# Projections of unnormalised tiles, the norm's inverse root applied to their results, and one sum over the squares

## What is computed

```python
def rms_norm(x, g):
    y = x * lax.rsqrt(jnp.mean(x * x, axis=-1, keepdims=True) + EPS)
    return y * g

for i in range(2):
    y = rms_norm(h, mix_norm[i])
    x_lru, g_lru, q, k, v, g_ret, u_sgu, v_sgu, g_sgu = split(y @ w_in[i])
    lru_out = rg_lru(conv(x_lru), ...)          # 4 taps, gates, a scan over the tokens
    ret_out = retention(q, k, v, ...)           # 6 heads, rotary q and k
    sgu_out = spatial_gating(u_sgu, v_sgu, ...)
    mixed = concatenate([lru_out * silu(g_lru), ret_out * silu(g_ret), sgu_out * silu(g_sgu)])
    h = h + mixed @ w_out[i]
    z = rms_norm(h, ple_norm[i])
    h = h + sigmoid(z @ w_ple_gate[i]) * (p[i] @ w_ple_proj[i])
h = rms_norm(h, final_norm)                     # then attention, then the experts
```

## Time and profile before

| | us |
|---|---|
| median of 3 runs (2720.45 to 2722.91) | 2721.89 |
| the profiled execution | 2722.76 |
| span of its trace | 2720.9 |
| PE busy / DVE busy / ACT busy / POOL busy | 2549.7 / 1837.7 / 1333.7 / 731.6 |
| layers 0 and 1 | 0 to 1070 |
| modulation and attention | 1070 to 1445 |
| experts | 1500 to the end |

### The profile page before, as it was taken

One profiled execution on the slowest core, in us unless ns is written; L12 is line 12 of the kernel. 1 busy time (PEld: TensorE's weight loads), 2 busy tenths in 40 slices (PEclk: granted clock), 3 DMA queues, 4 the chain that ended last, 5 costly groups with the idle time before them and its releaser, 6 DMA issues.

```text
span 2720.9 us, 32767 instructions
## 1 busy us (share of the span) xinstructions
PE 2549.7 (94%) x11541; PEld 2001.7 (74%) x11541; DVE 1837.7 (68%) x1658; ACT 1333.7 (49%) x1233; POOL 731.6 (27%) x402
## 2 busy tenths in 40 slices
PE   4999999989999988989896799999999999999995
PEld 2777787657777865678665688888888888888884
DVE  5478631264875123038524799999999999999995
ACT  3252233233322232123323577777777777777773
POOL 2333265233323632004321221122222121222120
PEclk8999999889999989999996899999999999999998
DMA  4233232132322323643102899999999999999993
GB/s 181 67 127 93 63 93 85 39 109 78 124 70 78 93 62 114 229 145 93 55 1 87 320 367 373 370 374 371 368 369 370 365 371 373 371 373 365 369 367 110
DMA packets 105359, 573.61 MB, mean 211 GB/s; under 512 B 14288, under 2 KB 14432, under 8 KB 55472
## 3 DMA queue, kind: packets, MB, share of 16 engines
q1 hardware_dynamic: 94416, 540.32, 53.4%
q0 software_dynamic: 10432, 31.81, 4.6%
q10 hardware_dynamic: 432, 0.40, 0.1%
HBM read 560.42 MB, written 24.12 MB: 215 GB/s over the span
## 4 chain that ended last, share of the span: by engine, by line
PE 90%; DVE 5%; ACT 1%; DMA 1%; DVEq 1%; issue 1%; POOL 0%; ACTq 0%; SPq 0%; POOLq 0%
PE ps L1465 87%; PE ps L1149 2%; DVE scr L1951 1%; DVEq L1955 1%; DVE scr L1931 1%; PE ps L623 0%; DMA pieces<-in_pieces 0%; POOL pieces_split L2142 0%; DMA scr<-in_positions 0%; DMA mix<-acc_rows 0%; PE ps L659 0%; DMA acc_rows<-rows,lst 0%; DVE scr L940 0%; DVE w_split L1276 0%; PE ps L1401 0%
## 5 line engine op out<-in xcount | busy, mean ns | idle before, releaser
L1276 DVE TENSOR_TENSOR w_split<-raw,w_split 128x2048 fp32r<-128x2048 f32 x386 | 877.6, 2288 | 54.3 <-ACT w_split L1228 43.4
L1465 PE MATMUL ps<-y_split,pieces_split 128*128 128x512 f32 x3600 | 854.8, 398 | 43.7 <-DVE y_split L1947 40.3
L1465 PEld LDWEIGHTS ps<-y_split,pieces_split 128*128 128x128 f32 x3600 | 682.6, 191 | 207.7 <-issue 44.7
L1228 ACT ACTIVATE w_split<-raw 128x2048 fp32r<-128x2048 f32 x386 | 736.3, 1917 | 197.3 <-PE ps L1465 177.3
L1465 PE MATMUL ps<-w_split,rows_T 128*128 128x512 f32 x3096 | 752.1, 394 | 1.9 <-DVE rows_T L1282 1.9
L1465 PEld LDWEIGHTS ps<-w_split,rows_T 128*128 128x128 f32 x3096 | 575.8, 189 | 118.8 <-DVE rows_T L1282 2.5
L2142 POOL TENSOR_TENSOR pieces_split<-pieces,pieces_split 128x1024 fp32r<-128x1024 f32 x172 | 420.0, 2445 | 878.9 <-ACT pieces_split L1713 571.0
L1713 ACT ACTIVATE pieces_split<-pieces 128x1024 fp32r<-128x1024 f32 x138 | 146.2, 1059 | 516.6 <-PE ps L1465 467.7
L1465 PE MATMUL ps<-w_split,hidden_T 128*128 128x512 f32 x1536 | 363.1, 392 | 1.7 <-DVE hidden_T L1282 1.7
L1465 PEld LDWEIGHTS ps<-w_split,hidden_T 128*128 128x128 f32 x1536 | 285.9, 188 | 72.1 <-DVE hidden_T L1282 13.9
L1340 POOL COPY rows_i<-slot_tokens 128x1 int32 (+1 forms) x34 | 59.2, 1742 | 409.4 <-PE ps L1149 375.5
(11 more groups left out here) (241 smaller groups left out, 2071.0 us busy)
## 6 DMA issues: line engine op xcount, KB each, us to landing
raw<-in_w_moe SPq DMA_DIRECT2D x386, 1024.0 KB, 7.4
pieces<-in_pieces SPq DMA_DIRECT2D x237, 512.0 KB, 3.7
acc_rows<-in_zeros POOLq DMA_DIRECT2D x5, 512.0 KB, 14.0
hT<-in_xT SPq DMA_DIRECT2D x8, 256.0 KB, 7.7
h_rows<-scr SPq DMA_DIRECT2D x4, 512.0 KB, 3.2
mix<-acc_rows SPq DMA_DIRECT2D x4, 512.0 KB, 5.0
out_T<-hT SPq DMA_DIRECT2D x8, 256.0 KB, 2.1
scr<-in_decay POOLq DMA_DIRECT2D x1, 1536.0 KB, 10.5
```

Source lines behind the costliest of these rows:

```text
L1228: nc.scalar.activation(wsp[:, p % SPLIT, 0], raw[:, p % RAW, :], ACT.Copy).then_inc(high, 3 if p == 1 else 1)
L1276: nc.vector.tensor_tensor(wsp[:, p % SPLIT, 1], raw[:, p % RAW, :], wsp[:, p % SPLIT, 0].bitcast(F32), ALU.subtract).then_inc(low, 3 if p ...
L1465: return pe.matmul(out, lhsT, rhs, start=start, stop=stop)
```

## The change

1. The tiles that are projected are `h * gain`, without the norm's factor. `gained_high` (ACT) and `gained_low` (DVE) make the two parts straight from `hT`.
2. The factor `rn` (the inverse root, the same on all partitions) is applied to results: `scale_gate` on DVE multiplies each gate's bank by `rn` before ACT's tanh; the convolution's first step multiplies xl by `rn` on its way out of PSUM, in place of ACT's copy; q and k by cos and sin tables that are multiplied by `rn` once (`ncos`, `nsin`); v and vs as the scale of ACT's copies, for which PE turns `rn` into columns by four tiny transposes into an A bank of their own (`rt`, placed between i2 and v0.0 in A's order) and ACT copies them to `rT`; u by a multiplication of the gate's product; g by `scale_ple`.
3. The first three projections of a norm go side by side over the tiles (`side_by_side`: xl0..xl2, g0..g2), nine matmuls for each tile.
4. DVE adds the eight squared tiles (`add_square`), and one matmul sums over the partitions (`norm_sum`), within the side-by-side part (after tile 7; in layer 1's opening after tile 3).
5. At the start: x and pieces are loaded in turns; the preparation of constants (decay rates, rotary tables) goes from before the first norm to between layer 0's convolutions; POOL issues its constant loads after its first weight pieces.
6. p and `w_ple_proj` come by one DMA into `work`; the raw places then hold only the next layer's pieces, and the next layer's first four pieces are split during g4..g7. The small products stand between g4..g7 and after them.

```diff
@@ layer_pieces
-    out += col(a, *(f"g{i}" for i in range(DK)))
-    out += [(f"ple{i}", False, v, f"p{DK - 1}") for i in range(4)]
+    out += col(v, "g0", "g1", "g2") + col(a, *(f"g{i}" for i in range(3, DK)))
@@ a_order
             a_order += [f"{w}{3 * g + m}" for m in range(3) for w in ("r", "i")]
+            a_order += ["rt"] if g == 0 else []
             a_order += [f"v{g}.{t}" for t in range(ST)]
@@ TensorE
-            for k in range(DK):
-                next_sum(-1, k)
+            def norm_sum(layer, g, n):
+                pe.wait_ge(sq_added, n)
+                pe.wait_ge(A.free, A.reusable(layer, g) if layer >= 0 else 1)
+                mm(ps[:, A.bank(g), :], ones[:], sq_sum, True, True).then_inc(A.full, 1)
...
+                def side_by_side(pool, names, first, sums):
+                    ws = [wps[:, L_AT[g] % A_SPLIT].rearrange("p c (k n) -> p c k n", k=DK) for g in names]
+                    for g in names:
+                        high_of(L_AT[g])
+                        low_of(L_AT[g])
...
+                    for k in range(DK):
+                        at_ = layer * 2 * DK + first + k + 1
+                        pe.wait_ge(yh_ready, at_)
+                        for g, w in zip(names, ws):
+                            mm(ps[:, pool.bank(g), :], w[:, 0, k, :], ys[:, 0, k, :], k == 0, False)
+                            mm(ps[:, pool.bank(g), :], w[:, 1, k, :], ys[:, 0, k, :], False, False)
+                        sums(k)
+                        pe.wait_ge(y_ready, at_)
+                        for g, w in zip(names, ws):
+                            m = mm(ps[:, pool.bank(g), :], w[:, 0, k, :], ys[:, 1, k, :], False, k == DK - 1)
...
+                def opening_sum(k):
+                    if k == (DK - 1 if layer == 0 else 3):
+                        norm_sum(layer - 1, "next", 2 * layer + 1)
+                side_by_side(A, ("xl0", "xl1", "xl2"), 0, opening_sum)
+                for name, _, pool, g in LAYER[3:12]:
+                    project(pools[pool], g)
@@ ScalarE
-                    nc.scalar.activation(mix[:, tile, :], full(V, g), ACT.Tanh, scale=0.5).then_inc(th_ready, 1)
+                    act.wait_ge(scaled, layer * 16 + i + 1)
+                    nc.scalar.activation(mix[:, tile, :], ps[:, V.bank(g), :], ACT.Tanh, scale=0.5).then_inc(th_ready, 1)
...
                     ahead("gl5" if g == 0 else "gr1")
                     for m in range(3):
                         act.wait_ge(la_ready, layer * 6 + 3 * g + m + 1)
                         nc.scalar.activation(mix[:, 6 + m, :], mix[:, 9 + m, :], ACT.Exp)
                         nc.scalar.activation(mix[:, 9 + m, :], mix[:, 9 + m, :], ACT.Tanh).then_inc(at_ready, 1)
+                    if g == 0:
+                        nc.scalar.activation(rT, full(A, "rt")[:, 0:8], ACT.Copy)
+                        act.drain().then_inc(A.free, 1)
@@ VectorE
-                r = inverse(7, std_ready, layer * NSTD + 8, std)
-                normalised(lambda k: p_("ple_norm", k), r, layer * 2 * DK + DK)
+                    if m >= 2:
+                        gained_low(m - 2, layer, DK, "ple_norm")
+                    if m >= 5:
+                        add_square(m - 4, layer * NSQ + 14, 14)
...
+                for i in range(3):
+                    conv(i)
+                if layer == 0:
+                    prep_one_plus()
+                scale_gate("gl0", 0)
+                conv(3)
+                silu2("gl0", 0, 0)
+                conv(4)
+                if layer == 0:
+                    prep_rate()
+                conv(5)
+                if layer == 0:
+                    prep_angles()
+                gates([f"gl{i}" for i in range(1, 6)], lambda i: 1 + i, 1)
```

More of the change, by code:

```diff
@@ L26 @@
 AX = mybir.AxisListType
-N_CONST = 6
+N_CONST = 5
 EPSC = 1e-6
@@ L715, in tail_act @@
             act.drain().then_inc(A.free, 1)
-            for i in range(1, A_SPLIT):
-                act.wait_ge(*landed(L, i))
-                nc.scalar.activation(wps[:, i, 0], pieces[:, i % A_RAW, :], ACT.Copy).then_inc(p_high, 1)
             for j in range(6):
@@ L1691, in squares, with root @@
                     nc.scalar.activation(buf[:, (first + k) % 2, 0:cols], tile(k), ACT.Square).then_inc(rd or sq_ready, 1)
-            def root(pool, g, layer, i, width, out, cols=S, ready=None, free=None, per=NSTD):
+            def root(pool, g, layer, i, width, out, cols=S, ready=None, free=None, per=HEADS):
                 act.wait_ge(pool.full, pool.done(layer, g))
```

538 lines of the change are left out of this document (330 added, 208 removed).

## The result

The changed kernel takes 2652.0 us (median of four runs, 2650.8 to 2652.9) against 2722.1 us: a ratio of 0.9743, 95% interval 0.9726 to 0.976. The forecast was 2659.5 us within 2640 to 2682, so the direction and the range hold, and the gain is 70 us where 62 was forecast. The profiled execution has a span of 2648.9 us against 2720.9, 72.0 less. The page first: span, instructions, and the chain that ended last by engine.

What follows compares the result with a forecast made beforehand. TensorE (PE) was taken as the bound, ending the chain last for 90% of the span. Terms 18.1 - 15.0 - 7.0 + 20.1 + 20.8 + 18.1 + 7.3 = 62.4; 2721.9 - 62.4 = 2659.5 us, range 2640 to 2682.

Steps and rivals of the forecast that it cites:

- Step 1: Opening to the end of gl5: TensorE starts at 18.0 us, later waits 14.7 us for gl1's bank; gain 18.1 us.
- Step 2: `rt` ahead of v0, each layer: v0.3 waits 5.6 us for the bank `rt` holds; loss 7.5 per layer, 15.0 us.
- Step 3: Where the heads begin, each layer: k0's high part and rotation come late; loss 3.5 per layer, 7.0 us.
- Step 4: `norm2`, each layer: 72 matmuls follow `wo` at once; gain 20.1 us in layer 0, 20.8 in layer 1.
- Steps 5 and 6: End of layer 0 to layer 1's xl2: gain 18.1 us; end of layer 1 to second modulation product: gain 7.3.
- The rest: Everything outside the six steps, such as u's factor, q, k, v and the DMA for p: no gain.
- The first rival, the covered queue: DVE is faster through the opening and v0.3 finds its bank: both together 2630 us, one alone 2644; chance 0.17.
- VectorE late in more places: VectorE 5 us later at gl5, layer 1's gl5 waits 5, both layer ends 4 more each: 2678 us; chance 0.20.
- the exposed hop of each gate: Each of 32 gates makes PE wait for its hops between PE, DVE and ACT; at 3 us, 2755 us; chance 0.03.

Runs made afterwards that it cites:

- The experiment with the angles: Changed kernel with VectorE preparing the rotary angles ahead of the first root's inverse instead of behind the last convolution: 2641.8 us (0.9701).

## Why the prediction was right, and where it was off

**Step 1, the opening: right mechanism, sizes off.** TensorE started at 17.74 (forecast 18.0). The idle before gl5 was 11.63 us and released by VectorE's `silu2`, as said; 14.7 was forecast. The term that was mis-sized is GpSimd's contention. I charged eight low parts 2.2 us each, 17.6 in all. VectorE and GpSimd in the changed kernel:

```profile
41.95 8.34 DVE L2100 SCALAR_TENSOR_TENSOR scr<-scr,par_all 128x512 f32<-128x512 f32 x3
...
61.93 6.37 DVE L2100 SCALAR_TENSOR_TENSOR scr<-scr,par_all 128x512 f32<-128x512 f32 x3
...
70.93 4.37 DVE L2100 SCALAR_TENSOR_TENSOR scr<-scr,par_all 128x512 f32<-128x512 f32 x3
...
39.17 10.56 POOL L2316 TENSOR_TENSOR pieces_split<-pieces,pieces_split 128x1024 fp32r<-128x1024 f32 x4 [5.38 <-ACT pieces_split L1805]
62.26 10.83 POOL L2316 TENSOR_TENSOR pieces_split<-pieces,pieces_split 128x1024 fp32r<-128x1024 f32 x4 [12.53 <-ACT pieces_split L1805]
```

Three operations take 2.40 us undisturbed; here 8.34, 6.37 and 4.37, which is 11.9 us more, and two TENSOR_SCALAR beside them 1.0 more: 12.9. The low parts came in two bursts of four that cost 6.4 us each, 1.6 for a part and not 2.2. That makes the chain 4.7 us shorter; the root came 1.0 earlier (inverse done at 39.89, forecast 40.9), and the rest of the chain took 38.7 us where 36.9 was forecast. So part of the error cancelled. None of the low parts came into the angles at all, because ScalarE was held at its own gate. The second mis-sized term is the clock: gl5 took 7.60 us, 2.2 above 5.4, where 1.5 was forecast. The experiment with the angles confirms that the rest of the chain counts us for us.

**Step 2, `rt` ahead of v0: right.** The wait was 4.84 and 4.73 us (forecast 5.6), the slow matmuls behind it cost a little more than forecast, the stretch lost 7.3 and 7.8 (forecast 7.5), and moving the copy takes back 6.7 and 7.3. What went unsaid is that this loss is needless: one copy stood in the wrong place of ScalarE's queue.

**Step 3, the heads: this step failed.** I forecast 3.5 us for each layer: the tanh of gr2, held back by its scaling, makes k0's high part late, and four more scalings make its rotation late. The wait is there (ScalarE idles until 198.92), but TensorE does not feel it. From gr2 to the scores it is 38.11 us as before, where 3.5 more was forecast. The high part of k0 is ready 24.8 us after gr2's start (forecast 29.1; TensorE wants it at 27.2), and the rotation ends at 213.40, 0.36 us ahead of the scores. The error is in the time at which I let VectorE's scan end. I took it from the kernel before, where the earlier trace rows show ScalarE released at 215.09, 26.6 us after gr2's start. In that number were three low parts of GpSimd that stretched three VectorE operations by about 2 us each. In the changed kernel the very wait that I priced keeps ScalarE's splits, and so all but the first of these parts, away from the scan: ScalarE is released 23.3 us after gr2's start. The experiment that puts the splits first brings the stretch back, 4.4 us on VectorE. A loss of 1.0 and 0.7 us stands instead between gr0 and gr2, most of it TensorE's wait of 0.77 and 0.42 us for a tanh of the second LRU group; it also stands behind gates that now wait for VectorE. The prediction did not name that place.

**Step 4, norm2: right.** 20.9 and 21.7 against 20.1 and 20.8, and no idle between `w_out` and g0. Its inside is clearer now: 6.0 us are the cheaper sum, and the overlap is worth 24 to 25, more than the whole, since VectorE's additions alone would have made the norm slower.

**Steps 5 and 6: right.** The waits were 5.48 (forecast 6.2) and 7.10 us; gains 17.7 against 18.1, and 6.1 against 7.3. (In step 5 VectorE's terms add up to 54.1, not 54.3 to 54.8; it changes nothing.) Both waits turned out to be avoidable by the order of TensorE's queue.

**The rest** was forecast at nothing and gave 1.6 us, and nothing seen ties it to the change. The largest piece is twelve matmuls at the end of the attention: 7.11 us in the kernel before, at a granted clock of 0.66 from 1385 to 1390 us, and 5.42 in the changed one at 1.00. The pauses ahead of them are the same (1.30, 1.02 and 0.90 us); why the clock fell in one of the two runs stays open.

The first rival, the covered queue, was half right in its reason (ScalarE is held by its own gate, and splits later), and most of the gain above the forecast (5.3 us at the heads, 3.0 in the opening) came from it. VectorE late in more places, and the exposed hop of each gate, did not come.

## What to carry to other kernels

A wait that is added to one queue also holds back all that this queue releases. Where that is a neighbour which steals time from the engine on the path, price the stretch with the neighbour gone, not as it was. When a normalisation is moved behind the products, put every step that does not need the root (angles, other products, the copy that frees a bank) ahead of the first one that waits for it: here that was worth 44 us more, against 70 for the change itself.
